# mLSTM value strips of the second block as seven block products, with strip and token sums mostly on GpSimd

## The chip, the cores and the metric

One core of one Trainium2 chip runs the whole program. The metric is the device time of one execution in microseconds (us). TensorE (PE in the rows) multiplies matrices and writes PSUM banks, ScalarE (ACT) does activation functions and copies out of PSUM, VectorE (DVE) does elementwise work, GpSimd (POOL) does elementwise work in SBUF and issues some DMAs, SyncE (SP) issues the weight DMAs.

## The reference, cut to what matters

Two blocks in a row; the first is not touched. In the second, the token mixer projects 256 context and 256 latent tokens (1024 features each) with one wide matrix and feeds the columns to two recurrences, mLSTM and HGRN2.

```python
def _token_mix(xc, xl, w_in, b_in, m_gain, lb, h_gain, proj_m, proj_h, w_out, need_ctx):
    seg_c = _split_proj(xc @ w_in + b_in)
    seg_l = _split_proj(xl @ w_in + b_in)
    hm_c, hm_l = _mlstm_branch(seg_c[0:6], seg_l[0:6], m_gain, xl.dtype)   # q, k, v, o, input gate, forget gate
    hh_c, hh_l = _hgrn_branch(seg_c[6:10], seg_l[6:10], lb, h_gain, xl.dtype)

# _mlstm_scan, one chunk: v enters here
    num = w_inter[..., None] * jnp.einsum('bhtd,bhdv->bhtv', qc, C) + jnp.einsum('bhts,bhsv->bhtv', s, vc)
```

There are 8 heads with 128 value columns each. The change is in `x @ w_in + b_in` for the 1024 value columns `v`, all in float32.

## The kernel before, in words

Every engine runs a list of instructions written out by hand, in order; semaphores (`S.…`) hold an engine until another has counted them up. `p.next` and `p.inc` keep the counts while the program is built. There is no scheduler. A float32 matmul of the program is two MATMUL instructions in the rows, each with its weight load, so counts in the profile are twice those in the code.

**The mLSTM phase** runs over four pairs of heads (`PAIRS`, counted from pair 0). For a pair four weight strips are loaded by SyncE: slot `W[0]` holds q and k, `W[1]` the 256 value columns `M_V`, `W[2]` the output gate, `W[3]` a gate strip of the other recurrence. A load waits for `S.done[r]`, which TensorE counts when it has read slot `r`. `U` holds the normalised tokens with features on the partitions: columns 0 to 255 latent, 256 to 511 context; `UP` is the latent part in column-major order.

TensorE's order in a pair is: `project` (q, k), `columns` of the pair before, `project_values`, then `remember` (scores, output gate tile 0, the state products, output gate tile 1, sums of head 0, gate strip, sums of head 1). The state products need `MV`, the biased values (`S.mv`), and `sums(h)` needs the decay tables `EE` (`S.e_ready`). In pair 0 `gate_columns` stands between the values and the scores; it transposes the gate rows `G4` and stops TensorE until VectorE has copied them (`S.tg_ready`).

**Values before:** 4 token tiles x 8 feature tiles, tokens stationary, 256 weight columns moving, into both halves of banks 2 and 3. VectorE then adds the bias `VB` while it moves them to `MV` (two instructions).

**The gate chain** of pair 0 runs beside `project` and the values: ScalarE and VectorE turn the raw gate rows (40 partitions) into cumulative sums (scans on 8 partitions) and maxima, until VectorE counts `S.gate_m`; ScalarE then makes the three exponentials of `G4` (`S.gate_exp`). GpSimd waits for that with four DMAs of gate rows to DRAM and the DMAs that broadcast them back into `WBN` and `WBX`, used by VectorE's `arguments`.

**Seven products.** The same trick that the change applies to the values already stands in other phases: for a strip split in 2 x 2 blocks (`part(t, h)`: output half t, feature half h), four weight sums (`WSR[0..3]`) and four token sums (`TBR[0..3]`) make seven block products do the work of eight. ScalarE must copy partial results out of a bank (`S.snap`) before TensorE adds a later product on top, and VectorE puts the parts together. `steps_f` of the phase after (the recurrence) does it with these buffers; its sums are made by GpSimd (weights) and by `token_sums` on VectorE (tokens, called once after pair 1).

Of the kernel before, what the change touches and what calls it, by code (L numbers as in the profile page):

```python
# [13 lines left out]
P = 128  # L14
# [242 lines left out]
def first_and_second_block(nc, a, out):  # L257
# [4 lines left out]
    with ctx:  # L262
# [168 lines left out]

        GMS, GHS = (v.rearrange("p a b c -> p (a b c)") if len(v.shape) == 4 else v.rearrange("p c d t x -> p (c d t x)")
# [39 lines left out]
        def permuted_and_context(h, c):  # L472

            return (UP[:, 4 * h:4 * h + 4, 0:SEQ], U[:, 4 * h:4 * h + 4, SEQ:2 * SEQ])[c]

# [255 lines left out]
        def _(eng):  # L731
# [665 lines left out]
            def project_values():  # L1397
                token_tiles(1, [(2, 0, toks(0)), (2, SW, toks(P)), (3, 0, toks(2 * P)), (3, SW, toks(3 * P))], (2, 3))
# [73 lines left out]
            p.leave("memory")  # L1472
            project(first=True)
            project_values()
# [165 lines left out]
            places["sums"] = (p.now(S.prod), p.now(S.wsum))  # L1640
# [76 lines left out]
        def _(eng):  # L1717
# [119 lines left out]

            eng.wait_ge(S.gate_exp, p.next(S.gate_exp))
# [5 lines left out]
            for i in range(PAIRS):  # L1844
                if i > 1:
                    eng.wait_ge(S.wb_used, p.next(S.wb_used))
# [3 lines left out]
                for h in range(2):  # L1850
                    src = rows_dram[1, 2 * i + h, :, :].rearrange("d x -> (d x)").partition_broadcast(DH)
                    eng.dma_start(WBX[i % 2][DH * h:DH * h + DH, :, :].rearrange("p d x -> p (d x)"), src).then_inc(sem, p.inc(sem, 16))

            p.meet("recurrence")
            prod, wsum = places["sums"]
            p.skip(S.prod, prod - p.now(S.prod))
            p.skip(S.wsum, wsum)
            for n in range(2 * PAIRS):
                r = n % 2
                part = lambda t, h: W[r][:, 4 * h:4 * h + 4, t * P:(t + 1) * P]  # L1860
                eng.wait_ge(S.land[r], p.next(S.land[r], 16))
                for o, x, y, op, used in ((0, part(1, 0), part(1, 1), ALU.add, 2), (1, WSR[0], part(0, 0), ALU.subtract, 2),
                                          (3, part(0, 1), WSR[1], ALU.subtract, 1), (2, part(0, 0), part(1, 0), ALU.subtract, 1)):
                    if n:
                        eng.wait_ge(S.prod, p.next(S.prod, used))
                    eng.tensor_tensor(WSR[o], x, y, op).then_inc(S.wsum, p.inc(S.wsum))  # L1866
                    eng.wait_ge(S.wsum, p.now(S.wsum))
# [3 lines left out]
        def _(eng):  # L1871
# [433 lines left out]
            act(GI[both, :], bank[6][both, :], ACT.Identity, bias=P2[both, B_IF:B_IF + 1]).then_inc(S.gate_in, p.inc(S.gate_in))  # L2305
            eng.wait_ge(S.gate_m, p.next(S.gate_m))
# [3 lines left out]
            eng.wait_ge(S.gate_exp, p.now(S.gate_exp))  # L2310

# [36 lines left out]
            for i in range(PAIRS):  # L2348
# [193 lines left out]
        def _(eng):  # L2542
# [623 lines left out]
            eng.memset(MV[:, :, :, P:VW], 1.0)  # L3166
            eng.memset(C0[:, :, :, :], 0.0).then_inc(S.order_dve, p.inc(S.order_dve))
# [54 lines left out]

            def arguments(i):
# [8 lines left out]
            for i in range(PAIRS):  # L3232
# [13 lines left out]
                ins.then_inc(S.mv, p.inc(S.mv))  # L3246
                eng.wait_ge(S.mv, p.now(S.mv))
                eng.sem_inc(S.free[2], 1)
                eng.sem_inc(S.free[3], 1)
# [303 lines left out]
```

## Time and profile before

| | us |
|---|---|
| three runs: lowest, median, highest | 1972.21, 1975.35, 1975.98 |
| the profiled execution: its own time | 1971.99 |
| the profiled execution: span of the core | 1970.2 |
| TensorE busy in the span | 1945.2 |
| VectorE, ScalarE, GpSimd busy | 1241.7, 565.9, 218.7 |

The span is the time from the core's first to its last instruction in the trace; the execution's own time is 1.8 us longer. All rows of the trace give times from the start of that span. An engine that is busy 99% of the span can still be the wrong place to look in one stretch: what matters is which wait ends last there.

### The profile page before, as it was taken

To read this page: it belongs to the slowest core of one execution; us is meant where nothing else is said; L and a number is where in the kernel's file an instruction comes from. 1 tells how busy PE (TensorE), PEld (TensorE's weight loads), DVE (VectorE), ACT (ScalarE), POOL (GpSimd) and SP (SyncE) were. 2 spreads that over 40 slices of the span, in tenths; PEclk is the share of its full clock that TensorE was granted. 3 is DMA by queue.
4 is the path that set the end of the run, shared out by engine and by line. 5 is a ranking of instruction groups with operands and counts; after the bars stand their busy time and mean duration, and the time that the engine had idled before them with its cause. 6 is when DMAs were issued, how large, how long until landed. Compare 5 with 4: busy or idle time off the path is not lost.

```text
span 1970.2 us, 31165 instructions
## 1 busy us (share of the span) xinstructions
PE 1945.2 (99%) x12449; PEld 1751.1 (89%) x12449; DVE 1241.7 (63%) x2513; ACT 565.9 (29%) x1363; POOL 218.7 (11%) x267
## 2 busy tenths in 40 slices
PE   9999999999999999999999999999999999999998
PEld 7878999977799998888888888888888989999998
DVE  5425897572378865899669565343456765766664
ACT  3343332224533313111110013322343323132212
POOL 6100430312014200000000001001212100000000
PEclk9999999999999999999999999999999999999999
DMA  6354555343545542555545364332222224545552
GB/s 199 112 187 137 165 165 161 111 151 114 172 150 171 182 140 79 182 166 164 166 152 173 116 190 136 119 90 86 86 65 67 83 67 148 172 134 167 171 177 81
DMA packets 272105, 273.60 MB, mean 139 GB/s; under 512 B 7982, under 2 KB 269338, under 8 KB 271962
## 3 DMA queue, kind: packets, MB, share of 16 engines
q1 hardware_dynamic: 270152, 267.65, 42.5%
q0 software_dynamic: 1216, 3.32, 0.6%
q8 instruction: 99, 1.62, 0.4%
q10 hardware_dynamic: 594, 0.65, 0.1%
q14 instruction: 44, 0.36, 0.1%
HBM read 270.38 MB, written 1.08 MB: 138 GB/s over the span
## 4 chain that ended last, share of the span: by engine, by line
PE 93%; DVE 4%; ACT 1%; issue 1%; DMA 1%; ACTq 0%; DVEq 0%; SPq 0%; PEldq 0%
PE bank L818 50%; PE bank L1324 10%; PE bank L796 8%; PE bank L1510 5%; PE bank L1559 2%; PE bank L966 2%; PE bank L1087 1%; PE bank L1610 1%; PE bank L1037 1%; PE bank L1494 1%; PE bank L1572 1%; PE bank L1046 1%; PE bank L1391 1%; PE bank L1235 1%; PE bank L1241 1%
## 5 line engine op out<-in xcount | busy, mean ns | idle before, releaser
L818 PE MATMUL bank<-arena,SQ 128*128 128x136 f32 (+2 forms) x2176 | 341.4, 308 | 0.1
L818 PEld LDWEIGHTS bank<-arena,SQ 128*128 128x128 f32 x2176 | 307.0, 191 | 17.2 <-ACT arena L1931 0.3
L818 PE MATMUL bank<-arena,W 128*128 128x136 f32 (+2 forms) x1824 | 272.6, 301 | 2.7 <-issue 2.1
L818 PEld LDWEIGHTS bank<-arena,W 128*128 128x128 f32 x1824 | 247.6, 191 | 15.4 <-issue 4.1
L1931 ACT ACTIVATE H<-bank 128x128 f32<-128x128 f32 (+1 forms) x260 | 82.3, 317 | 535.5 <-PE bank L818 535.5
L818 PE MATMUL bank<-U,W 128*128 128x136 f32 (+2 forms) x1296 | 194.6, 303 | 0.0
L818 PEld LDWEIGHTS bank<-U,W 128*128 128x128 f32 x1296 | 176.4, 191 | 11.0 <-issue 2.9
L796 PE MATMUL bank<-U,W 128*128 128x272 f32 (+1 forms) x576 | 133.1, 392 | 1.4 <-ACT U L2213 0.8
L3033 DVE SCALAR_TENSOR_TENSOR W<-W,CC 128x256 f32<-128x256 f32 x280 | 128.3, 483 | 7.0
L796 PEld LDWEIGHTS bank<-U,W 128*128 128x128 f32 x576 | 109.0, 190 | 24.6 <-issue 2.3
L818 PE MATMUL bank<-arena 128*128 128x136 f32 (+1 forms) x1024 | 124.1, 278 | 0.0
L818 PEld LDWEIGHTS bank<-arena 128*128 128x128 f32 x1024 | 120.6, 191 | 0.0
L1324 PE MATMUL bank<-W,U 128*128 128x256 f32 (+1 forms) x512 | 100.5, 355 | 0.0
L818 PE MATMUL bank<-U,SQ 128*128 128x136 f32 (+2 forms) x608 | 98.2, 304 | 0.0
L1931 ACT ACTIVATE arena<-bank 128x136 f32<-128x136 f32 x176 | 49.3, 280 | 168.9 <-PE bank L818 168.9
L1324 PEld LDWEIGHTS bank<-W,U 128*128 128x128 f32 x512 | 86.8, 190 | 11.5 <-issue 2.0
L818 PEld LDWEIGHTS bank<-U,SQ 128*128 128x128 f32 x608 | 85.9, 191 | 4.1
L1822 POOL TENSOR_TENSOR SQ<-W 128x512 f32<-128x512 f32 x32 | 40.7, 1273 | 267.9 <-PE bank L818 267.9
L1866 POOL TENSOR_TENSOR W<-W 128x512 f32<-128x512 f32 x32 | 41.7, 1302 | 255.4 <-PE bank L1510 170.7
L2932 DVE SCALAR_TENSOR_TENSOR arena<-arena,PL 128x270 f32<-128x270 f32 x72 | 62.7, 871 | 2.6
L1842 POOL DMA_DIRECT2D gate_rows<-arena x4 | 2.1, 540 | 528.7 <-ACT arena L2309 528.7
L2121 ACT ACTIVATE arena<-arena,PL 128x272 f32<-128x272 f32 x80 | 41.8, 522 | 64.5 <-DVE arena L2781 56.6
(459 smaller groups left out, 3117.9 us busy)
## 6 DMA issues: line engine op xcount, KB each, us to landing
W<-in_ffn_w_up_dram SPq DMA_DIRECT2D x44, 1024.0 KB, 5.1
W<-in_ffn_w_in_dram SPq DMA_DIRECT2D x44, 1024.0 KB, 5.1
W<-in_ada_w_dram SPq DMA_DIRECT2D x36, 1024.0 KB, 6.6
W<-in_mix_w_in_dram SPq DMA_DIRECT2D x36, 1024.0 KB, 5.3
W<-in_ffn_w_down_dram SPq DMA_DIRECT2D x16, 1408.0 KB, 6.6
W<-in_ffn_w_out_dram SPq DMA_DIRECT2D x16, 1408.0 KB, 6.3
W<-in_w_in_dram SPq DMA_DIRECT2D x21, 1024.0 KB, 5.3
W<-in_w_out_dram SPq DMA_DIRECT2D x8, 1024.0 KB, 8.5
```

Source lines behind the costliest of these rows:

```text
L796: last = mm(bank[b][0:m, 0:n], W[r][:, kk, t * P:t * P + m], rhs(kk), start=kk == 0, stop=kk == k - 1)
L818: last = mm(o, a(k), b[:, k], start=not adds and k == 0, stop=k == kt - 1, skip_group_check=True)
L966: return mm(bank[2 * (r % 2) + t][:, c0:c0 + n], W[r][:, k, t * P:(t + 1) * P], rhs(k), start=k == 0, stop=k == KD - 1, skip_group_check=True)
L1324: last = mm(o, x, y, start=i == 0, stop=i == n - 1 and bias is None, skip_group_check=True)
L1510: ins = mm(o, x, y, start=clear and k == 0, stop=k == 3, skip_group_check=True)
L1559: last = mm(bank[b][:, c:c + SW], tok(k), W[r][:, k, :], start=k == 0, stop=k == KD - 1, skip_group_check=True)
L1822: eng.tensor_tensor(WS[n % 2][:, 0], part(1, 0), part(1, 1), ALU.add).then_inc(S.order_pool, p.inc(S.order_pool))
L1866: eng.tensor_tensor(WSR[o], x, y, op).then_inc(S.wsum, p.inc(S.wsum))
L1931: act(sn[:, i, :], bank[b][:, c:c + w], ACT.Copy).then_inc(S.snap, p.inc(S.snap))
L2121: act(CZ[:, 2 * s + t, :], Z[:, g % 2, 2 * s + t, :], ACT.Copy, scale=PLs[l][:, c:c + 1]).then_inc(S.tap, p.inc(S.tap))
L2932: stt(CZ[:, i, 2:], Z[:, g % 2, i, 0:T1 - 2], w(0), CZ[:, i, 2:], ALU.mult, ALU.add).then_inc(sem, p.inc(sem))
L3033: ins = stt(o, x, c, o, ALU.mult, ALU.add) if k else ts(o, x, c, None, ALU.mult)
```

## The change

Each of the four calls of `project_values` becomes seven block products. A block product is 4 feature tiles x 2 token tiles, tokens stationary, 128 weight columns moving: 56 matmuls of 128 columns for 32 of 256. The raw value copies `SNV` (made by ScalarE in `kept_values`) get their bias on VectorE and are then added to what stands in the banks. The weight sums of the value strips, and three of the four token sums, are made by GpSimd; the first token sum of all is VectorE's, ahead of the gate chain. The token sums of the recurrence move from VectorE (after pair 1) to GpSimd (after pair 3). The diff, shortened:

```diff
+        SNV = [SQ[:, 4 + i // 2, (i % 2) * SEQ:(i % 2 + 1) * SEQ] for i in range(4)]
+        SNV_LATE = SQ[:, 5, :].rearrange("p (a b) -> p a b", a=2)
...
-            def project_values():
-                token_tiles(1, [(2, 0, toks(0)), (2, SW, toks(P)), (3, 0, toks(2 * P)), (3, SW, toks(3 * P))], (2, 3))
+            def project_values(first=False):
...
+                def product(b, c, tok, w, clear=False, release=False):
+                    for k in range(4):
+                        for n in range(2):
+                            last = mm(bank[b][:, c + n * P:c + (n + 1) * P], tok[:, k, n * P:(n + 1) * P], w[:, k],
+                                      start=clear and k == n == 0, stop=k == 3, skip_group_check=True)
+                        if release and k == 0:
+                            last.then_inc(S.done[1], p.inc(S.done[1]))
+                    return last
...
+                product(2, near, latent_and_context(0, 0), raw(0, 0), True).then_inc(S.prod, p.inc(S.prod))
+                take(3)
+                token_sum()
+                eng.wait_ge(S.wsum, p.next(S.wsum))
+                product(3, near, TBR[0], WSR[0], True).then_inc(S.prod, p.inc(S.prod))
+                eng.wait_ge(S.snap, p.next(S.snap))
+                product(2, far, latent_and_context(1, 0), raw(0, 1))
+                eng.wait_ge(S.snap, p.next(S.snap))
+                token_sum(2)
+                product(3, far, TBR[3], raw(1, 1)).then_inc(S.prod, p.inc(S.prod))
...
             project(first=True)
-            project_values()
+            project_values(True)
...
+            def strip_sums(r, which=(0, 1, 3, 2), first=False):
...
+            eng.wait_ge(S.done[3], p.next(S.done[3]))
+            strip_sums(1, (0,), True)
+            eng.wait_ge(S.tsum, p.next(S.tsum))
+            token_sum(1, latent_and_context(1, 1), TBR[0])
+            token_sum(3, latent_and_context(1, 0), TBR[1])
+            strip_sums(1, (1, 3), True)
+            token_sum(2, latent_and_context(1, 1), latent_and_context(0, 1))
+            strip_sums(1, (2,), True)
             eng.wait_ge(S.gate_exp, p.next(S.gate_exp))
...
             for i in range(PAIRS):
                 if i > 1:
+                    strip_sums(1)
                     eng.wait_ge(S.wb_used, p.next(S.wb_used))
...
+            strip_sums(1)
+            eng.wait_ge(S.prod, p.now(S.prod) + 6)
+            eng.tensor_tensor(TBR[0], permuted_and_context(0, 1), permuted_and_context(0, 0), ALU.subtract).then_inc(S.order_pool, p.inc(S.order_pool))
...
+            kept_values((0,))
             eng.wait_ge(S.gate_m, p.next(S.gate_m))
...
             eng.wait_ge(S.gate_exp, p.now(S.gate_exp))
+            kept_values((1,))
...
                 eng.sem_inc(S.free[0], 1)
+                kept_values((0, 1, 2, 3) if i else (2, 3))
...
+            tt(TBR[0], latent_and_context(0, 1), latent_and_context(0, 0), ALU.subtract).then_inc(S.tsum, p.inc(S.tsum))
...
-                eng.wait_ge(S.done[1], p.next(S.done[1]))
-                vb = VB[:, i * SW:(i + 1) * SW].rearrange("p (b c) -> p b c", b=2).unsqueeze(1).to_broadcast([P, 2, 2, P])
-                for n in range(2):
-                    ins = tt(MV[:, 2 * n:2 * n + 2, :, 0:P], bank[2 + n][:, :].rearrange("p (a b c) -> p a b c", a=2, b=2), vb, ALU.add)
+                for n, t in ((0, 0), (3, 1), (1, 0), (2, 1)):
+                    eng.wait_ge(S.snap, p.next(S.snap))
+                    bias = VB[:, i * SW + t * P:i * SW + (t + 1) * P].unsqueeze(1).to_broadcast([P, 2, P])
+                    ins = tt(two_tiles(SNV[n]), two_tiles(SNV[n]), bias, ALU.add)
...
+                tt(MV[:, 2:4, 0, 0:P], two_tiles(SNV[1]), two_tiles(bank[3][:, 0:SEQ]), ALU.add).then_inc(S.order_dve, p.inc(S.order_dve))
...
+                tt(MV[:, 0:2, 0, 0:P], two_tiles(SNV[0]), two_tiles(bank[2][:, SEQ:2 * SEQ]), ALU.add)
+                both = two_tiles(bank[2][:, 0:SEQ]).unsqueeze(1).to_broadcast([P, 2, 2, P])
+                tt(MV[:, :, 1, 0:P].rearrange("p (c n) m -> p c n m", c=2), SNV_LATE.rearrange("p c (n m) -> p c n m", n=2), both,
+                   ALU.add).then_inc(S.mv, p.inc(S.mv))
...
-                if i == 1:
-                    token_sums(permuted_and_context, TBR)
...
-                r = n % 2
-                part = lambda t, h: W[r][:, 4 * h:4 * h + 4, t * P:(t + 1) * P]
...
+                strip_sums(n % 2)
```

**TensorE in pair 0**, from the last instructions of `project` to the scores (`bank<-W,U` is weights and tokens of the program; names after "waits" are semaphores). Before:

```order
L1324 MATMUL bank<-W,U 128x128 x16
L1324 MATMUL bank<-W,U 128x256 [waits free3,free2,land1]
L1324 MATMUL bank<-W,U 128x256 x31
L1366 MATMUL bank<-ident,arena 128x40 [waits free4,gate_exp]
L1366 MATMUL bank<-ident,arena 128x40 x7
L1408 MATMUL bank<-arena 128x256 [waits free4,free5,mqk,tg_ready]
```

After (of the eight instructions of each product the first stands here):

```order
L1331 MATMUL bank<-W,U 128x128 x16
L1414 MATMUL bank<-W,U 128x128 [waits free2,land1]
L1414 MATMUL bank<-W,H 128x128 [waits wsum,tsum,free3]
L1414 MATMUL bank<-W,U 128x128 [waits snap]
L1414 MATMUL bank<-W,arena 128x128 [waits tsum,snap]
L1414 MATMUL bank<-W,H 128x128 [waits wsum]
L1414 MATMUL bank<-W,U 128x128 [waits wsum]
L1414 MATMUL bank<-W,arena 128x128 [waits snap,wsum,tsum]
L1373 MATMUL bank<-ident,arena 128x40 [waits free4,gate_exp]
L1454 MATMUL bank<-arena 128x256 [waits free4,free5,mqk,tg_ready]
```

The values' one wait for slot 1 and the banks has become seven groups of eight, each with a wait of its own: on weight sums (`wsum`), token sums (`tsum`) or ScalarE's copies (`snap`). `tsum,snap` is the fourth product.

**GpSimd**, from the last strip of the first block to its DMAs of gate rows. Before:

```order
L1822 TENSOR_TENSOR SQ<-W 128x512 [waits prod,land3,first_sums]
L1824 TENSOR_TENSOR SQ<-W 128x512 [waits order_pool]
L1842 DMA gate_rows<-arena 8x256 [waits gate_exp,prod,first_sums]
L1842 DMA gate_rows<-arena 8x256 x3
L1849 DMA arena<-gate_rows 128x1024 [waits wrow]
L1852 DMA arena<-gate_rows 64x512 x2
L1849 DMA arena<-gate_rows 128x1024
```

After (`H<-U,H`, `arena<-U,H` and `arena<-U` are token sums of 1024 elements, `W<-W` weight sums of 512):

```order
L1870 TENSOR_TENSOR SQ<-W 128x512 [waits order_pool]
L1904 TENSOR_TENSOR W<-W 128x512 [waits done3,land1,prod,first_sums]
L1891 TENSOR_TENSOR H<-U,H 128x4x256 [waits tsum,wsum]
L1891 TENSOR_TENSOR arena<-U,H 128x1024 [waits tsum]
L1904 TENSOR_TENSOR W<-W 128x512 [waits tsum]
L1904 TENSOR_TENSOR W<-W 128x512 [waits wsum]
L1891 TENSOR_TENSOR arena<-U 128x1024 [waits wsum]
L1904 TENSOR_TENSOR W<-W 128x512 [waits tsum]
L1919 DMA gate_rows<-arena 8x256 [waits gate_exp,wsum]
L1919 DMA gate_rows<-arena 8x256 x3
L1927 DMA arena<-gate_rows 128x1024 [waits wrow]
```

Seven sums now stand between the last strip of the first block (L1870) and the DMAs of gate rows. Further down, the four weight sums of pair 1's strip stand ahead of the DMA for pair 2.

**ScalarE in pair 0**, the gate chain's end. After the change:

```order
L2380 ACTIVATE arena<-bank,P 40x512 [waits gf_full]
L2387 ACTIVATE SQ<-bank 128x256 [waits prod]
L2393 ACTIVATE arena<-arena 40x256 [waits gate_m]
L2394 ACTIVATE arena<-arena 40x256
L2395 ACTIVATE arena<-arena 40x256
L2387 ACTIVATE SQ<-bank 128x256 [waits prod,gate_exp]
L1956 ACT_TABLE_LOAD
L2437 ACTIVATE arena<-bank,MQB 128x256 [waits done0]
L2438 ACTIVATE arena<-bank,P 128x256
L2387 ACTIVATE SQ<-bank 128x256 [waits mqk,prod]
L2387 ACTIVATE SQ<-bank 128x256 [waits prod]
```

The four copies `SQ<-bank` are new. The second of them, which the fourth product waits for, stands behind the three exponentials (40x256) and so behind `gate_m`; the last two stand behind q and k.

## Rows read from the trace of the kernel before

**Rows 1.** The page: busy time, the granted clock in 40 slices, the chain by engine

```profile
PE 1945.2 (99%) x12449; PEld 1751.1 (89%) x12449; DVE 1241.7 (63%) x2513; ACT 565.9 (29%) x1363; POOL 218.7 (11%) x267
...
PEclk9999999999999999999999999999999999999999
...
PE 93%; DVE 4%; ACT 1%; issue 1%; DMA 1%; ACTq 0%; DVEq 0%; SPq 0%; PEldq 0%
```

**Rows 2.** The chain that ended last in 1185 to 1262 us: start, us, what

```profile
1192.44 17.39 PE bank L1324 x96
1209.83 0.63 PE bank L1366 x8
...
1239.64 3.57 PE bank L1324 x32
...
1243.64 13.81 PE bank L1324 x64
```

**Rows 3.** Timeline of the merge phase: start, us, engine, line, operation, count

```profile
1648.95 1.06 PE L818 MATMUL bank<-W 128*128 128x128 f32 x8
1649.85 1.06 PE L818 MATMUL bank<-U,arena 128*128 128x128 f32 x8
```

**Rows 4.** Timeline of the gate chain in pair 0

```profile
1186.89 0.60 ACT L2295 ACTIVATE arena<-bank 128x512 f32<-128x512 f32 x1 [2.26 <-PE bank L1338]
...
1187.90 0.49 DVE L3167 MEMSET arena<- 128x516 f32 x1
...
1190.49 0.74 DVE L3170 TENSOR_SCALAR arena<-bank,P 40x512 f32<-40x512 f32 x1 [2.10 <-ACT arena L2299]
...
1191.74 0.68 DVE L3174 TENSOR_TENSOR arena<-arena 40x512 f32<-40x512 f32 x1 [0.51 <-ACT arena L2303]
...
1192.46 2.55 DVE L3181 TENSOR_TENSOR_SCAN arena<-ones_row,arena 8x256 f32<-8x256 f32 x4
1195.18 0.69 DVE L3185 TENSOR_TENSOR arena<-arena 40x512 f32<-40x512 f32 x1 [0.17 <-DVE arena L3181]
...
1199.53 0.51 ACT L2307 ACTIVATE arena<-arena 40x256 f32<-40x256 f32 x1 [7.25 <-DVE arena L3206]
...
1200.35 0.40 ACT L2309 ACTIVATE arena<-arena 40x256 f32<-40x256 f32 x1
...
1201.35 2.14 POOL L1842 DMA_DIRECT2D gate_rows<-arena  x4 [528.67 <-ACT arena L2309]
```

**Rows 5.** Timelines: elementwise work of GpSimd and a token sum of VectorE

```profile
357.11 0.73 POOL L1835 TENSOR_TENSOR HIB<-HIB 128x256 f32<-128x256 f32 x1
...
1285.54 1.22 DVE L2701 TENSOR_TENSOR H<-U,H 128x1024 f32<-128x1024 f32 x1
...
1342.13 5.29 POOL L1866 TENSOR_TENSOR W<-W 128x512 f32<-128x512 f32 x4 [80.50 <-DMA W<-in_mix_w_in_dram]
```

**Rows 6.** Timelines: VectorE and GpSimd at the same time, and VectorE alone

```profile
346.90 1.91 DVE L2764 TENSOR_TENSOR arena<-W 128x1408 f32<-128x1408 f32 x1 [0.22 <-DVE arena L2787]
...
347.41 1.99 POOL L1835 TENSOR_TENSOR HIB<-HIB 128x256 f32<-128x256 f32 x1
...
1415.64 1.30 DVE L3407 TENSOR_TENSOR_SCAN arena<-arena,ones_row 128x255 f32<-128x255 f32 x2
...
1424.39 2.30 DVE L3410 TENSOR_TENSOR_SCAN arena<-arena,ones_row 128x255 f32<-128x255 f32 x2
...
1424.68 1.46 POOL L1866 TENSOR_TENSOR W<-W 128x512 f32<-128x512 f32 x1 [23.25 <-PE bank L1510]
```

**Rows 7.** Timeline of TensorE at the start of the program

```profile
2.84 4.56 PE L747 MATMUL bank<-ident 128*128 128x128 f32 x20 [2.84 <-POOL LNT L1730]
```

**Rows 8.** Timeline behind the values of pair 0, and the landing of the load issued there (last number)

```profile
1212.64 1.28 DVE L3245 TENSOR_TENSOR arena<-bank,arena 128x512 f32<-128x512 f32 x2
...
1216.11 1.59 PE L1324 MATMUL bank<-arena 128*64 128x129 f32 x16
...
W<-in_mix_w_in_dram SPq DMA_DIRECT2D x1, 1024.0 KB, 6.2
```

More of the change, by code:

```diff
@@ L1472, in _ @@
             p.leave("memory")
+            places["sums"] = (p.now(S.prod), p.now(S.wsum), p.now(S.tsum))
             project(first=True)
-            project_values()
+            project_values(True)
             gate_columns()
@@ L1836, in _, with token_sum @@
                         eng.wait_ge(sem, p.now(sem))
+            p.meet("memory")
+            prod, wsum, tsum = places["sums"]
+            p.skip(S.prod, prod - p.now(S.prod))
+            p.skip(S.wsum, wsum)
+            p.skip(S.tsum, tsum)
+            def token_sum(o, x, y):
+                eng.tensor_tensor(TBR[o], x, y, ALU.subtract).then_inc(S.tsum, p.inc(S.tsum))
+                eng.wait_ge(S.tsum, p.now(S.tsum))
+            def strip_sums(r, which=(0, 1, 3, 2), first=False):
+                part = lambda t, h: W[r][:, 4 * h:4 * h + 4, t * P:(t + 1) * P]
+                for o in which:
+                    if o == 0:
+                        eng.wait_ge(S.land[r], p.next(S.land[r], 16))
+                    x, y, op, used = ((part(1, 0), part(1, 1), ALU.add, 2), (WSR[0], part(0, 0), ALU.subtract, 2),
+                                      (part(0, 0), part(1, 0), ALU.subtract, 1), (part(0, 1), WSR[1], ALU.subtract, 1))[o]
+                    if not first:
+                        eng.wait_ge(S.prod, p.next(S.prod, used))
+                    eng.tensor_tensor(WSR[o], x, y, op).then_inc(S.wsum, p.inc(S.wsum))
+                    eng.wait_ge(S.wsum, p.now(S.wsum))
+            eng.wait_ge(S.done[3], p.next(S.done[3]))
[6 more added lines that the diff above has]
+            strip_sums(1, (2,), True)
             eng.wait_ge(S.gate_exp, p.next(S.gate_exp))
@@ L1852, in _ @@
                     eng.dma_start(WBX[i % 2][DH * h:DH * h + DH, :, :].rearrange("p d x -> p (d x)"), src).then_inc(sem, p.inc(sem, 16))
+            strip_sums(1)
+            eng.wait_ge(S.prod, p.now(S.prod) + 6)
+            eng.tensor_tensor(TBR[0], permuted_and_context(0, 1), permuted_and_context(0, 0), ALU.subtract).then_inc(S.order_pool, p.inc(S.order_pool))
+            eng.wait_ge(S.order_pool, p.now(S.order_pool))
+            eng.tensor_tensor(TBR[1], permuted_and_context(1, 1), TBR[0], ALU.subtract).then_inc(S.order_pool, p.inc(S.order_pool))
+            eng.wait_ge(S.order_pool, p.now(S.order_pool))
+            token_sum(3, permuted_and_context(1, 0), TBR[1])
             p.meet("recurrence")
[L1855 to L1857 removed]
             for n in range(2 * PAIRS):
[L1859 to L1867 removed]
+                strip_sums(n % 2)
         @block.scalar
@@ L2305, in _, with kept_values @@
             act(GI[both, :], bank[6][both, :], ACT.Identity, bias=P2[both, B_IF:B_IF + 1]).then_inc(S.gate_in, p.inc(S.gate_in))
+            def kept_values(which):
+                x, z, y = bank[2][:, 0:SEQ], bank[3][:, 0:SEQ], bank[3][:, SEQ:2 * SEQ]
+                for n in which:
+                    eng.wait_ge(S.prod, p.next(S.prod, 2 if n == 2 else 1))
+                    i, src = ((0, x), (3, z), (1, x), (2, y))[n]
+                    act(SNV[i], src, ACT.Copy).then_inc(S.snap, p.inc(S.snap))
+                    if n == 3:
+                        p.skip(S.prod)
+            kept_values((0,))
             eng.wait_ge(S.gate_m, p.next(S.gate_m))
```

33 lines of the change are left out of this document (29 added, 4 removed).

## The prediction

> **What bounds the kernel now.** The page comes first. TensorE is busy 99% of the span and carries 93% of the chain that ended last [rows 1]. So the question in each stretch is only whether TensorE's stream gets shorter, and whether something new stops it. VectorE (63%) and GpSimd (11%) look idle enough to take any work, but these are averages; what counts is who waits for them in the stretch of the change.
>
> The chain in order of time then shows the mLSTM phase as one stream of TensorE. In pair 1 the values are 64 instructions in 13.81 us, 0.216 us each, and the 32 instructions of 128 columns before them take 3.57 us, 0.1116 us each [rows 2]. In pair 0 both kinds stand in one piece: 96 instructions in 17.39 us, from 1192.44 to 1209.83. The values of pair 0 thus begin near 1192.3 + 3.57 = 1195.85 and end near 1209.7.
>
> **What the change takes from TensorE.** A call of `project_values` becomes 112 instructions of 128 columns. The nearest rows for such block products are those of the merge phase: eight in 1649.85 - 1648.95 = 0.90 us, 0.1116 us each as above, with semaphore waits between the groups and no gap [rows 2, 3]. 112 x 0.1116 = 12.50 us for 13.81 to 13.82: 1.32 us less per call, **-5.3 us** in four calls. One block in eight is saved, but under a tenth of the time, because two instructions of 128 columns take 0.223 us where one of 256 takes 0.216.
>
> **Pair 0: sums that come before the gate chain is done.** The other places where the stream could stop are the seven new groups of waits. Pair 0 is the tight one, since the sums can't be made in an earlier pair.
>
> VectorE's first token sum (1024 elements, 1.22 us [rows 5]) stands ahead of the `MEMSET` that began at 1187.90. VectorE waited 2.10 us before 1190.49 for ScalarE [rows 4], and the sum fits into that: it costs nothing. Were the cover gone, it would be 1.2 us.
>
> GpSimd starts at about 1186.9, when `done[3]` starts ScalarE as well [rows 4]. A weight sum takes 5.29 / 4 = 1.32 us with its gap, 1.27 without [rows 5, 6]. No row shows a GpSimd sum of 1024 elements. From 0.73 us at 256 and 1.27 at 512 I work out 0.73 + 3 x 0.54 = 2.35 us; the bounds are 1.27 and 2 x 1.32 = 2.64. The order is: weight sum to 1188.2, wait for VectorE's token sum to 1189.4, token sum to 1191.8, then 2.35 + 1.27 + 1.27 + 2.35 + 1.27 = 8.5 us more, to 1200.8. By themselves all are in time for TensorE: products 2 to 7 follow in steps of 16 x 0.1116 = 1.79 us, the fourth at 1195.85 + 3 x 1.79 = 1201.2, the seventh at 1206.6.
>
> But GpSimd's sums run exactly while VectorE works on the gate chain, and the rows show that the two hold each other up. Two scans take 1.30 us alone, and 2.30 us when a GpSimd sum of 1.27 us asks during the first: it got in between the two though VectorE had no wait there. A GpSimd operation of 0.73 us took 1.99 us beside a VectorE operation with two SBUF inputs [rows 5, 6]. So they alternate, one operation each, at +1.00 us for a sum of 1.27 us, that is its duration less 0.27. From 1191.74 VectorE has six operations that read two SBUF tiles: one `TENSOR_TENSOR`, four scans, one `TENSOR_TENSOR` (L3174, L3181, L3185) [rows 4]. That is five gaps for GpSimd's five sums. Delay: 8.5 - 5 x 0.27 = 7.15 us; the first may be partly hidden in VectorE's own wait, I take 7.0. Bounds: 0 if these operations, on 40 and 8 partitions, don't collide (every case in the rows has 128), and 8.5 + 0.6 if nothing overlaps.
>
> Here a rule is weighed against the rows. The Trainium skill, page "SBUF — State Buffer", section "Who interferes with whom", says that a VectorE instruction with two SBUF inputs and a GpSimd instruction that reads SBUF contend for a shared port, held for the whole instruction. Nothing in it depends on the number of partitions. By the rule the delay is the 7 us above; by the rows alone it lies between 0 and 9. The rule speaks against this change, and the trace agrees with it as far as it goes.
>
> **What waits for the gate chain.** Before, ScalarE's exponentials started at 1199.53 and ended at 1200.75; only the gate DMAs and the transposes behind the values needed them [rows 4]. Now the copy of bank 3 (`kept_values((1,))`) stands behind them on ScalarE, and the fourth product waits for it. With the chain 7.0 us late the copy ends at 1200.75 + 7.0 + 0.4 = 1208.15 (0.4 us as the last exponential). TensorE, in order, is at that product at 1201.2. **+7.0 us** of stop, with products 4 to 7, transposes and scores queued behind. Without the collision the copy would be ready at 1201.15, and the stop nothing.
>
> **The clock after the stop.** TensorE has not stood still for as long as this anywhere but at the program's start. There, behind 2.84 us without work, 20 instructions of 128 columns took 4.56 us, 0.228 us each, twice the 0.1116 of later: the 1.2 GHz level for the 2.4 GHz level [rows 7]. (The granted-clock line prints its highest digit in all slices and does not resolve this [rows 1].) If the stop brings the clock down in the same way and 4.4 us of work follow at the lower level, half of that is lost: **+2.2 us**. Bounds: 0 if it stays up, 7.1 us (products 4 to 7 at double) if it stays down for all four. The Trainium skill, page "TensorE: Matmul & The Clock Gate", Part 1, calls the throttled state the default that activity releases; by it the clock falls, and the sum holds the 2.2 us, without it the sum is 2.2 us less.
>
> **Behind the values of pair 0.** VectorE has four bias additions on SBUF, two additions of 256 and one of 512 elements where it had two of 512 in 1.28 us [rows 8]. From 0.42 us for the first and 0.34 for each that follows, about 1.7 + 0.5 + 1.1 = 3.3 us: `MV` is ready 2.0 us later than before against the end of the values. It was ready at 1213.9, TensorE took it at 1216.11 [rows 8]: slack 2.2 us, cost 0, by a hair. In pairs 1 to 3 the four additions are made while the products still run, so nothing is later than before.
>
> GpSimd's gate DMAs leave 7 us later than 1201.35 [rows 4], but the values end later by more than 6 as well; their users follow `MV`. Cost 0.
>
> **Pair 3 and the recurrence.** Three token sums (7.1 us) and four weight sums (5.3 us) begin at the end of pair 3's values, about 1344 in the new time, and end near 1357. The recurrence wants them from about 1372. Cost 0; the four token sums taken from VectorE (4.9 us at 1285.54 [rows 5]) give nothing, as no engine waited for them.
>
> **The sum.** -5.3 + 7.0 + 2.2 = **+3.9 us** on the profiled execution's 1971.99 us, 1975.9. The runs shown have their median 3.4 us above that execution, so on their scale 1975.35 + 3.9 = **1979.2 us**. A measurement of this kernel can tell about 0.2% from no change, 3.95 us: the forecast lies on that line, from below.
>
> **Rivals.**
> 1. *No collision in the gate chain* (operations on few partitions don't block, or GpSimd always loses and keeps its slack of 5.8 us before the seventh product). For it: no row shows a blocked operation with fewer than 128 partitions. Against: the scans on 128 alternate. Only the -5.3 us are left: 1970.1, faster. The turning point is a delay of 5.3 us with the clock up, of 3.1 with it down. Chance 0.22.
> 2. *The stop, but the clock stays up*: -5.3 + 7.0 = +1.7, 1977.1. Chance 0.13.
> 3. *A short stop* of 1 to 5 us without the clock's fall, because VectorE often gets in twice running: -4 to 0. Chance 0.05, counted as no change.
> 4. *A second collision at `MV`*. The strip of pair 1 is asked for in the last product, about 1.1 us before the values end, and lands 6.2 us later [rows 8], so 5.1 us behind the end. The additions run from 3 to 6 us behind it. If it lands a little earlier, up to three of them wait one weight sum each: +1 to +3.8 us on the likeliest case, 1981 to 1983. The same chance holds a clock that stays down for longer. Chance 0.15.
>
> The likeliest case has 0.45, its own range is +2.7 to +5.6 us (a 1024-element sum of 1.9 to 2.6 us, 1.5 to 3.4 us for the clock). Half of it lies over 0.2%. Faster: 0.22. Slower: 0.22 + 0.15 = 0.37. Same: 0.41. The range reaches from rival 1 to rival 4: 1969.5 to 1983.5.
>
> **What the new profile would show.** Block products of the values at 0.11 us each, 12.5 us from first to last in pairs 1 to 3, with no gap. In pair 0, one idle time of about 7 us before a group that reads `W` and `arena` (the fourth product), put down to ScalarE; the scans, 2.55 us before, spread over 8 us or more with GpSimd's sums between them; the first instructions behind the stop at 0.22 us. If the scans still take 2.55 us, rival 1 is right. If TensorE waits at the state products (`bank<-arena` 128x129), rival 4 is. The forecast would be wrong altogether if GpSimd's sums of 1024 elements took far longer than 2.6 us, or if the block products ran slower than in the merge phase.

## The result, and the profile after

The changed kernel takes 1976.57 us (median of 19 runs, 1975.65 to 1980.6), the kernel before 1972.38 us beside it (19 runs, 1971.85 to 1975.98): ratio 1.002 [1.0013, 1.0028]. It is slower by 4.2 us; the interval leaves out 1, so the loss is real, and it is about 0.2%. The profiled execution has a span of 1974.6 us, 4.4 more than before.

The page of the changed kernel, as in [rows 1]:

```profile
PE 1942.4 (98%) x12641; PEld 1755.4 (89%) x12641; DVE 1263.2 (64%) x2530; ACT 572.0 (29%) x1379; POOL 257.6 (13%) x289
...
PE 94%; DVE 2%; ACT 1%; DMA 1%; issue 1%; ACTq 0%; DVEq 0%; SPq 0%; PEldq 0%
```

TensorE has 2.8 us less work, and VectorE 21.5 us more although it lost token sums and gained only small additions. The additions explain little of it: they take 2.9 us for 1.28 in each pair, and of the token sums 1.2 us came and 4.9 us left, 3 us more in all. That is the first sign: operations that were there before became longer.

Timeline of pair 0, the stretch of [rows 4] (start, us, engine, line, operation). L3265, L3272, L3276 are the two-input operations and scans of the gate chain, L1904 and L1891 GpSimd's strip and token sums, L2387 the copies on ScalarE, L1414 the block products:

```profile
1187.32 3.11 POOL L1904 TENSOR_TENSOR W<-W 128x512 f32<-128x512 f32 x1 [514.50 <-PE bank L1345]
...
1188.10 1.21 DVE L3256 TENSOR_TENSOR H<-U 128x1024 f32<-128x1024 f32 x1
...
1190.51 2.37 POOL L1891 TENSOR_TENSOR H<-U,H 128x1024 f32<-128x1024 f32 x1
...
1192.04 1.39 DVE L3265 TENSOR_TENSOR arena<-arena 40x512 f32<-40x512 f32 x1 [0.51 <-ACT arena L2378]
...
1192.96 2.68 POOL L1891 TENSOR_TENSOR arena<-U,H 128x1024 f32<-128x1024 f32 x1
1193.46 8.63 DVE L3272 TENSOR_TENSOR_SCAN arena<-ones_row,arena 8x256 f32<-8x256 f32 x4
1195.72 3.14 POOL L1904 TENSOR_TENSOR W<-W 128x512 f32<-128x512 f32 x2
...
1198.94 2.61 POOL L1891 TENSOR_TENSOR arena<-U 128x1024 f32<-128x1024 f32 x1
...
1201.63 1.53 POOL L1904 TENSOR_TENSOR W<-W 128x512 f32<-128x512 f32 x1
...
1202.27 1.43 DVE L3276 TENSOR_TENSOR arena<-arena 40x512 f32<-40x512 f32 x1 [0.17 <-DVE arena L3272]
...
1207.36 0.51 ACT L2393 ACTIVATE arena<-arena 40x256 f32<-40x256 f32 x1 [8.84 <-DVE arena L3297]
...
1208.61 0.38 ACT L2387 ACTIVATE SQ<-bank 128x256 f32<-128x256 f32 x1
1209.04 3.78 PE L1414 MATMUL bank<-W,arena 128*128 128x128 f32 x16 [7.37 <-ACT SQ L2387]
...
1212.62 2.05 PE L1414 MATMUL bank<-W,H 128*128 128x128 f32 x16
1214.50 1.95 PE L1414 MATMUL bank<-W,U 128*128 128x128 f32 x16
```

Read it from below. The fourth product waited 7.37 us, for the copy at 1208.61. The copy stood behind ScalarE's exponentials, which started at 1207.36 where they had started at 1199.53. They waited for VectorE, whose four scans took 8.63 us instead of 2.55, and the operations before and after them 1.39 and 1.43 us instead of 0.68 and 0.69. GpSimd worked all that time. (The trace lies 0.3 us later than that of before from the start of this stretch.)

The last four products of pair 0, behind the stop, and the seven of pair 1, which run freely (the chain, as in [rows 2]):

```profile
1209.04 9.19 PE bank L1414 x64
...
1252.05 12.51 PE bank L1414 x112
```

The balance: 13.81 - 12.51 = 1.30 us saved in each pair; in pair 0 the transposes behind the values begin at 1218.17 instead of 1209.76, which is 8.1 us later after the 0.3. So +8.1 - 3 x 1.30 = +4.2 us.

### The profile page after: what moved, and what is told of

The parts are those of the page before. It is cut to its first block, busy times and chain, and to the rows that moved or that the text cites. A ratio compares the mean times of both kernels' runs of the same rounds, so it can differ in the third digit from the quotient of the medians.

```text
span 1974.6 us, 31636 instructions
## 1 busy us (share of the span) xinstructions
PE 1942.4 (98%) x12641; PEld 1755.4 (89%) x12641; DVE 1263.2 (64%) x2530; ACT 572.0 (29%) x1379; POOL 257.6 (13%) x289
## 3 DMA queue, kind: packets, MB, share of 16 engines
q0 software_dynamic: 1216, 3.32, 0.5%
## 4 chain that ended last, share of the span: by engine, by line
PE 94%; DVE 2%; ACT 1%; DMA 1%; issue 1%; ACTq 0%; DVEq 0%; SPq 0%; PEldq 0%
PE bank L825 52%; PE bank L803 9%; PE bank L1331 7%; PE bank L1557 5%; PE bank L1606 3%; PE bank L1414 2%; PE bank L973 2%; PE bank L1657 2%; PE bank L1044 1%; PE bank L1541 1%; PE bank L1094 1%; PE bank L1619 1%; PE bank L1053 1%; PE bank L1242 1%; PE bank L1248 1%; PE bank L1398 1%
## 5 line engine op out<-in xcount | busy, mean ns | idle before, releaser
L1904 POOL TENSOR_TENSOR W<-W 128x512 f32<-128x512 f32 x48 | 65.2, 1358 | 756.1 <-PE bank L1345 514.5
L825 PE MATMUL bank<-arena,U 128*128 128x256 f32 (+1 forms) x352 | 59.2, 327 | 0.4 <-DVE U L2852 0.4
L1557 PE MATMUL bank<-H,W 128*128 128x256 f32 x256 | 58.9, 379 | 0.7 <-ACTq L2471 0.7
L825 PEld LDWEIGHTS bank<-arena,U 128*128 128x128 f32 x352 | 53.5, 191 | 5.2 <-DVE U L2852 0.6
```

The lines of the kernel that those rows point to most:

```text
L825: last = mm(o, a(k), b[:, k], start=not adds and k == 0, stop=k == kt - 1, skip_group_check=True)
L1557: ins = mm(o, x, y, start=clear and k == 0, stop=k == 3, skip_group_check=True)
```

## The experiments

All medians below have the kernel before measured beside them (1972.1 to 1972.4 us); each ratio is to it.

**Theory A**, the prediction's: GpSimd's sums stretch VectorE's gate chain, ScalarE's copy waits for it, TensorE for the copy, and the clock falls. The rivals are lettered B, C and so on; a letter does not mean the same in every experiment, and each expectation says what it stands for.

### 1. The clock: work for TensorE in the stop

```diff
                 product(2, far, latent_and_context(1, 0), raw(0, 1))
+                if first:
+                    keep_busy(bank[5][:, 0:P], 28)
```

> 28 matmuls (56 instructions of 128 columns) that nobody reads stand between the third and the fourth product of pair 0, 56 x 0.1116 = 6.2 us of work inside a stop of 7.4 us. Theory A with the clock as the price of the stop: the idle time shrinks to about 1.2 us, the granted clock stays at 1.00, the products behind run at 0.112 us each: 1.9 us under the changed kernel, 2.3 us over the kernel before. Rival (the 0.22 us per instruction behind the stop belongs to these products, not to the clock): they stay slow and the time is that of the changed kernel.

Measured: 1974.49 us (11 runs), ratio 1.0012 [1.0003, 1.002], 2.1 us under the changed kernel. Windows of the changed kernel (stretch, its length, busy time and instructions of PE, PEld, DVE, ACT and POOL, then the granted clock as a share of 2.4 GHz, the DMA share and GB/s):

```profile
1183.00:1201.00 18.00, 18.00 (x127) 14.62 (x126) 16.06 (x28) 5.42 (x11) 13.29 (x6) 1.00 0.39 114
1201.00:1207.50 6.50, 0.68 (x7) 0.48 (x5) 5.88 (x13) 0.14 (x1) 2.08 (x2) 0.88 0.05 12
1207.50:1209.00 1.50, 0.00 (x0) 0.00 (x0) 0.00 (x0) 1.46 (x4) 0.00 (x0) 0.50 0.00 0
1209.00:1211.00 2.00, 1.96 (x9) 1.96 (x10) 0.00 (x0) 1.98 (x3) 1.85 (x4) 0.50 0.04 8
1211.00:1216.00 5.00, 5.00 (x39) 5.00 (x39) 0.00 (x0) 0.53 (x2) 3.57 (x7) 0.82 0.39 125
```

and of the kernel with the filler:

```profile
1201.00:1208.00 7.00, 6.56 (x59) 6.37 (x58) 5.52 (x13) 1.00 (x3) 1.70 (x2) 1.00 0.02 4
1208.00:1213.00 5.00, 4.32 (x38) 4.33 (x39) 0.00 (x0) 3.10 (x6) 2.83 (x6) 1.00 0.03 7
```

Without work the clock went to its 1.2 GHz level (0.50) during the stop, and stayed there for the first group behind it: 3.78 us for 16 instructions, then 2.05, then 1.95. With the filler it stayed at 2.4 GHz and the last four products took 7.41 us in one piece instead of 9.19. The clock's term is shown, and the rival falls: the same products ran at full speed. The copy that they wait for comes no earlier than before, so the rest of the loss stays.

### 2. One more sum on GpSimd

```diff
+            eng.tensor_tensor(TBR[1], latent_and_context(1, 1), TBR[0], ALU.subtract).then_inc(S.order_pool, p.inc(S.order_pool))
+            eng.wait_ge(S.order_pool, p.now(S.order_pool))
             token_sum(1, latent_and_context(1, 1), TBR[0])
```

> GpSimd makes the second token sum of pair 0 twice (2.37 us more of GpSimd work beside the gate chain). Theory A: the stop grows by 2.37 less 0.3 to about 9.5 us, the clock's loss stays: 2.1 us over the changed kernel, 6.3 us over the kernel before. Theory C: no change against the changed kernel, since the sums have 4 us of slack before the product that reads them.

Measured: 1977.64 us (7 runs), ratio 1.0027 [1.0016, 1.0038]: 1.1 us over the changed kernel, half of what theory A said. The timeline says why:

```profile
1201.32 2.60 POOL L1891 TENSOR_TENSOR arena<-U 128x1024 f32<-128x1024 f32 x1
1201.96 2.51 DVE L3278 TENSOR_TENSOR arena<-arena 40x512 f32<-40x512 f32 x1 [0.18 <-DVE arena L3274]
...
1204.00 1.59 POOL L1904 TENSOR_TENSOR W<-W 128x512 f32<-128x512 f32 x1
...
1209.89 3.78 PE L1414 MATMUL bank<-W,arena 128*128 128x128 f32 x16 [8.51 <-ACT SQ L2389]
```

VectorE has six operations beside which a sum can get in. The extra sum takes one place, and the last sum (1.27 us by itself) falls behind the sixth, where it delays next to nothing: 2.35 - 1.27 = 1.1 us. The stop grew by as much, from 7.37 to 8.51 us; the medians alone, with intervals that overlap, would not carry this. Theory C, no change at all, does not fit the longer stop. It is the prediction's alternation; my expectation forgot that its places are few.

### 3. The sums without their size

```diff
-                eng.tensor_tensor(TBR[o], x, y, ALU.subtract)
+                eng.tensor_tensor(cut_to(TBR[o]), cut_to(x), cut_to(y), ALU.subtract)
```

`cut_to` takes `v[:, :, 0:1]`, and the strip sums of pair 0 are cut alike, as is one token sum of the recurrence. Every wait stays; two products that read a token sum in the change read tokens here, and one of the recurrence reads another token sum. A first version, which left the operands of these products as they were, gave no time.

> The changed kernel with the sums of the mLSTM stage cut to their first element of each 128, all their waits kept (its values are therefore not the reference's): the collision is gone, everything else of the change stays. Theory A/D: the gate exponentials end near 1201, no stop before the fourth product of more than 0.5 us, the gate rows are as early as before, and all four value groups give 1.31 us each: 1972.3 - 5.3 = 1967.0 us (1966.5 to 1968). Rival B (the stop comes from the copy's place behind the gate exponentials, collision or not): a stop of 1 to 2 us and a lower clock stay, 1969 to 1971 us. Rival C (the saving is not there): 1971 us or more.

Measured: 1967.34 us (7 runs), ratio 0.9973 [0.9962, 0.9984]. The scans took 2.55 us again, and all seven products of pair 0 stand in one piece of the chain (the first line is from the timeline):

```profile
1194.39 2.55 DVE L3274 TENSOR_TENSOR_SCAN arena<-ones_row,arena 8x256 f32<-8x256 f32 x4
...
1197.95 12.61 PE bank L1414 x112
```

So the loss goes with the length of the sums. The waits, the copy's place, the longer additions and the seven products themselves leave 0.3 us by the medians, which these runs do not resolve (the interval is 2.2 us wide on each side), and 0.1 us in the trace, where the seven products take 12.61 us for 12.51 in pair 1. Rivals B and C of this experiment fall.

### 4. The copies first

```diff
-            kept_values((0,))
+            kept_values((0, 1, 2, 3))
             eng.wait_ge(S.gate_m, p.next(S.gate_m))
...
             eng.wait_ge(S.gate_exp, p.now(S.gate_exp))
-            kept_values((1,))
...
-                kept_values((0, 1, 2, 3) if i else (2, 3))
+                if i:
+                    kept_values((0, 1, 2, 3))
```

> In pair 0 all four of ScalarE's copies of the values stand ahead of its wait for the gate chain, so no product waits for the chain; the sums on GpSimd stay. Theory A (GpSimd's sums hold up VectorE's operations with two SBUF inputs, and the copy behind the chain hands that delay to TensorE): the four scans stay stretched to 8 to 9 us, the stop of 7.4 us before the fourth product goes, and with it the slow clock; perhaps 0.3 us before the transposes and 0.4 us before the scores, since q and k are copied later. Time 4.7 us under the kernel before, 8.9 us under the changed one. Theory B (the products themselves, or the token sums as operands, are slow in pair 0): the fourth product still starts late or runs at 0.22 us per instruction, and the time stays within 2 us of the changed kernel.

Measured: 1971.48 us (11 runs), ratio 0.9992 [0.9983, 1.0001]. The stop before the fourth product is gone, and the product runs at full speed, so this experiment's rival B falls. But of the 5.3 us only 0.7 are there, and the expected 4.7 us were missed. The chain shows another path, through the gate rows that go to DRAM and come back to VectorE's exponent arguments (L3322):

```profile
1211.33 2.60 DMA gate_rows<-arena
...
1215.34 4.75 DMA arena<-gate_rows
...
1220.12 3.95 DVE arena L3322 x8
```

and its timeline, GpSimd's strip sums and the first head's sums of TensorE:

```profile
1217.46 5.53 POOL L1904 TENSOR_TENSOR W<-W 128x512 f32<-128x512 f32 x4
...
1226.73 4.11 PE L1331 MATMUL bank<-arena 128*128 128x129 f32 x20 [1.94 <-DVE arena L3369]
```

TensorE stopped 1.94 us before the first head's sums and ran them at a low clock (0.58 granted over 1226.7 to 1230.8 us), 4.11 us for 2.40; with 0.45 us more before the scores that is 4.1 of the 4.6 us that were missing. Two things made it late: the gate rows, whose first transfer was issued at 1209.70 instead of 1201.35, 7.5 us later after the 0.8 us by which this trace lies later, and GpSimd's strip sums of pair 1, which the change put ahead of its next transfers and which ran beside the arguments. Theory A had neither; a theory D took the first.

### 5. The same collision in the kernel before

```diff
+            part = lambda t, h: U[:, 4 * h:4 * h + 4, t * P:(t + 1) * P]
...
+            extra(WSR[0], part(1, 0), part(1, 1), ALU.add)
+            eng.wait_ge(S.extra, 1)
+            extra(TBR[1], u(1, 1), TBR[0], ALU.subtract)
+            extra(TBR[3], u(1, 0), TBR[1], ALU.subtract)
...
             eng.wait_ge(S.gate_exp, p.next(S.gate_exp))
```

The strip sums have their size but read tokens here, not weights.

> The kernel before, with VectorE's first token sum and GpSimd's seven sums of pair 0 added at their places and sizes (four strip sums of 512 elements, three token sums of 1024); nobody reads them and no matrix product waits for them. All readings say that VectorE's gate chain is stretched by some 7.5 us, so that the gate exponentials end near 1208.5 in place of 1200.8 while the tokens-stationary values end at 1209.8. Theory A (the prediction's: the delay costs only through the ScalarE copy behind it, which this kernel does not have): no change, 1972.3 us within 1. Theory D (from the run with the copies first: the same delay has a second victim, the gate rows that go through DRAM to VectorE's exponent arguments, and with them the first head's sums): the arguments start near 1219.5 in place of 1214.2, TensorE stops 2 to 2.4 us before the first head's sums and loses another 1.7 to the clock, 1975.8 to 1976.4 us.

Measured: 1973.03 us (11 runs), ratio 1.0003 [0.9994, 1.0012]. The timeline (L3201 are the scans, L3248 the arguments, L1325 the first head's sums):

```profile
1192.99 8.64 DVE L3201 TENSOR_TENSOR_SCAN arena<-ones_row,arena 8x256 f32<-8x256 f32 x4
...
1219.53 1.92 DVE L3248 TENSOR_SCALAR arena<-arena 128x256 f32<-128x256 f32 x8 [5.07 <-DMA arena<-gate_rows]
...
1225.18 2.40 PE L1325 MATMUL bank<-arena 128*128 128x129 f32 x20
```

Its scans took 8.64 us and its exponentials began at 1206.94, so the gate chain was as late as in the changed kernel, and the time did not change beyond its interval. Theory D falls. Its late rows came as worked out (arguments at 1219.53), but the arguments took 1.92 us here, since the kernel before has no strip sums there, and the masks were ready at 1224.02 for a TensorE that came free at 1225.2. So experiment 4's stop needed both late rows and strip sums beside the arguments, and a TensorE that is not itself 8 us late: theory E, which the next experiment tests.

### 6. Those strip sums later, three times

First, on the kernel of experiment 4, they go behind the gate row transfers of pair 2:

```diff
                 if i > 1:
-                    strip_sums(1)
+                    if i > 2:
+                        strip_sums(1)
                     eng.wait_ge(S.wb_used, p.next(S.wb_used))
...
+                if i == 2:
+                    strip_sums(1)
```

> The version with all four ScalarE copies of pair 0 ahead of the gate exponentials, and one thing more: GpSimd makes pair 1's strip sums behind its gate row transfers of pair 2, about 1226, instead of ahead of them, 1217 to 1223. Theory E (the stop before the first head's sums in that version needed two things, gate rows late by the stretched chain and VectorE's arguments stretched from 1.92 to 3.95 us by those strip sums; the kernel before with the sums alone had only the first and no stop): arguments back at 1.92 us, masks ready about 1224.6 on that version's scale where TensorE comes free at 1224.8, no stop and no slow clock there, 3.5 to 4 us less than 1971.5: 1967.5 us (1967.2 to 1968.4). Rival F (the late gate rows alone make the stop): the arguments cannot begin before 1220, so at least 1.9 us of it stays, 1969.5 to 1971.5 us.

Measured: 1971.96 us (11 runs), ratio 1.0 [0.9991, 1.0009]; no gain, and outside what either theory had given. The first stop is gone as theory E said, and a second stands in its place (timeline; L3372 are the masks):

```profile
1222.77 2.28 DVE L3372 TENSOR_TENSOR arena<-arena,tri 128x256 f32<-128x256 f32 x2
1223.47 5.46 POOL L1904 TENSOR_TENSOR W<-W 128x512 f32<-128x512 f32 x4
...
1226.37 2.84 DVE L3372 TENSOR_TENSOR arena<-arena,tri 128x256 f32<-128x256 f32 x2
...
1233.43 3.51 PE L1331 MATMUL bank<-arena 128*128 128x129 f32 x20 [2.08 <-DVEq L3408]
```

The strip sums now ran beside the masks (0.76 us for each two of them alone), and the second head's sums were late.

Second, on top of this, the second token sum goes from GpSimd to VectorE, behind the first one:

```diff
+            tt(TBR[1], latent_and_context(1, 1), TBR[0], ALU.subtract).then_inc(S.tsum, p.inc(S.tsum))
```

> The previous version of this call, with the second token sum (the tokens' difference from the first) on VectorE at once behind the first, in the time in which it waits for the gate projection, instead of on GpSimd. GpSimd's row of sums is one of 2.4 us shorter, so the gate chain is stretched by some 5 us instead of 7.5, and ends near 1206. Theory E: the wait of 0.45 us before the score products goes too and the first head's sums have some 2 us to spare: 1967.0 us, 0.2 to 0.6 below the previous version, at the edge of what five rounds tell. Rival F: 1.5 to 2.5 us below the previous version, since the stop that it sees in the late rows shrinks with the chain.

Measured: 1972.65 us (11 runs), ratio 1.0001 [0.9992, 1.001], no better. The gate chain did end 0.7 us earlier, but the exponentials did not start earlier (1207.09 for 1207.14): with the four copies first, ScalarE's last copy waits for the sixth product at 1206.8. And the sum took 2.17 us on VectorE, beside GpSimd's strip sum. Neither theory had seen that. TensorE stopped 2.36 us before the second head's sums here too.

Last, GpSimd waits until VectorE has finished pair 0's first head:

```diff
                 if i == 2:
+                    eng.wait_ge(S.hm, 1)
                     strip_sums(1)
```

> The version with the four copies first, with pair 1's strip sums later still: GpSimd waits for VectorE to finish the first head of pair 0 (about 1232) before it makes them, 1232 to 1238; they are needed at 1248. Both earlier places cost the same 4 us: at 1217 to 1223 they stretched the exponent arguments (stop before the first head), at 1223 to 1229 the masks (0.76 to 2.28 and 2.84 us; stop of 2.1 us before the second head, and a low clock behind it). Theory E2 (every one of those stops is the late gate chain plus the strip sums beside VectorE's two-input operations; without the second there is none): arguments 1.92, masks 0.76 each, no stop before either head, 1967.5 us (1967.1 to 1968.6), level with or just below the version with pairs 1 to 3 only. Rival F2 (the late gate rows alone are enough to stop the second head's sums, or the sums behind 1232 make the stop before the columns' transposes): 1969.5 us or more.

Measured: 1968.86 us (11 runs), ratio 0.9984 [0.9975, 0.9993]: 3.1 us less than the first placing of this series, with nothing changed but the time of four sums. It lies 0.3 us over E2's range and below F2's. The two heads (timeline):

```profile
1224.63 2.47 PE L1331 MATMUL bank<-arena 128*128 128x129 f32 x20 [0.35 <-issue]
...
1230.83 2.47 PE L1331 MATMUL bank<-arena 128*128 128x129 f32 x20 [0.28 <-DVEq L3409]
```

Theory E2 is right in kind. Some 1.5 us of small waits stay: from the last 32 instructions of pair 0's `project` to those of pair 1's, the chain takes 47.43 us here and 47.20 in the kernel before, where the saving alone would give 45.90. Of these, 0.45 us lie before the scores and about 0.5 at each head's sums. The late rows make VectorE's chain the bound there, so F2 holds for that part.

### 7. The change without pair 0

```diff
             def project_values(first=False, sums_new=False):
+                if first:
+                    token_tiles(1, [(2, 0, toks(0)), (2, SW, toks(P)), (3, 0, toks(2 * P)), (3, SW, toks(3 * P))], (2, 3))
+                    return
```

Pair 0's copies and GpSimd's sums go, its biases are added as before; VectorE makes three token sums behind the gate chain. Pair 1's strip sums stand behind the gate row transfers of pair 2, as in the first placing of experiment 6.

> A version meant to beat both: pair 0 computes its values as before (four token tiles, biases added in one step), pairs 1 to 3 by the seven products. GpSimd does nothing beside the gate chain; VectorE makes the token sums, the first at its place and three behind the gate chain where it waits 11 us for the transposes; GpSimd makes pair 1's strip sums behind its first gate row transfers of pair 2. Theory A/D: no stop in pair 0, three times 1.31 us saved, 1972.3 - 3.9 = 1968.4 us (1967.8 to 1969.2). Rival: GpSimd's strip sums, now at 1218 to 1224, stretch VectorE's decay products and make the first head's sums late: 1970 us or more. Rival C (the saving of the seven products is eaten in pairs 1 to 3 too): 1971 to 1972.5 us.

Measured: 1968.18 us (11 runs), ratio 0.9978 [0.9969, 0.9986]. This beats both kernels, the one before by 4.2 us and the changed one by 8.4. Three pairs of 1.30 us make 3.9 of the 4.2. GpSimd's strip sums stretched the masks in pair 0 here too (2.29 and 2.85 us), but nothing waited (timeline):

```profile
1218.53 5.47 POOL L1908 TENSOR_TENSOR W<-W 128x512 f32<-128x512 f32 x4
...
1221.44 2.85 DVE L3383 TENSOR_TENSOR arena<-arena,tri 128x256 f32<-128x256 f32 x2
...
1224.58 2.40 PE L1331 MATMUL bank<-arena 128*128 128x129 f32 x20
```

> The version with seven products in pairs 1 to 3 only, its strip sums of pair 1 at the same later place. There its gate chain is early, so the masks that they stretched at 1218 to 1224 (2.29 and 2.85 us in place of 0.76) stopped nothing. Theory E2: same time as that version, 1968.2 us within 0.5. Rival (the stretched masks cost it something, through a late release of banks): 0.5 to 1 us less.

Measured, with `eng.wait_ge(S.hm, 1)` before those sums: 1968.11 us (11 runs), ratio 0.9977 [0.9967, 0.9986], the same. With an early gate chain the place of these sums is free.

## Why the prediction was right

It gave +3.9 us on the profiled execution; that became +4.4 in span and +4.2 in the medians. The mechanism it named is the one that the traces show; two of its terms came out as they did partly by luck (the clock's size and the gate DMAs, below). By its steps:

- **The saving**, -1.32 us a call: measured 1.30 in each of pairs 1 to 3, and -5.0 for all four in experiment 3. Right.
- **The collision**, 7.0 us by alternation of one operation each: the last of the six operations counted (L3276) ended at 1203.70 instead of 1195.87, 7.5 us later after the 0.3. The 1024-element sum took 2.37 us for an estimated 2.35. The doubt whether operations on 40 and 8 partitions collide is settled: they do, as those of 128. The Trainium skill, "SBUF — State Buffer", "Who interferes with whom", states the contention for a VectorE instruction with two SBUF inputs, without a condition on partitions; the trace agrees, with a scan on 8 partitions that went from 0.64 us to 2.2 us on average. Experiment 3 shows that the loss goes with the length of the sums, and experiment 2 that the chain has few places for them.
- **Where the 0.5 us more came from.** VectorE's first token sum was put at nothing, because VectorE waits there; that wait did cover it. But GpSimd's first strip sum ran beside it and took 3.11 us where 1.27 was taken. The second sum began at 1190.51 where 1189.4 was worked out, 0.8 us later after the 0.3, and so still held up L3265 (1.39 us for 0.68). The five sums of the prediction's account delayed the other five operations by 6.8 us, for its 7.15.
- **The stop**, +7.0: 7.4. Its path, through the copy behind the exponentials, was the one named; experiment 4 removed just this link, and the stop went.
- **The clock**, +2.2: 2.0 (9.19 - 7.14 us), and 2.1 by experiment 1. The estimate took 4.4 us of slow work from the program's start. That this would carry over to a stop in mid-stream no row had shown; the size is a lucky hit.
- **Costs put at nothing.** The additions before `MV`: it was ready at 1224.09, TensorE took it at 1224.52, so 0.4 us of slack were left; right, by a hair. Rival 4's collision there did not come: the strip sums began at 1223.55, after the four additions on SBUF; the last three additions have one input in PSUM, and the one beside which the sums began took 0.68 us, as in experiment 3 without them. The strip sums hit the arguments behind it instead (5.48 us for 1.93), and no stop of TensorE followed, for TensorE was itself 8 us late.
- **The gate DMAs**, cost 0, was right only because the stop hid them. "Their users follow `MV`" was the reason given, and it was thin: once the stop is gone (experiments 4 and 6) late rows and strip sums together took 4.6 to 5.2 us of the 5.3. The number 0 held for this kernel, the reason for it did not.
- **The recurrence's sums**, cost 0: right, with other times than given. They ran from 1354.07 to 1367.26, not from 1344 to 1357 (the sum of the prediction itself puts the end of pair 3's values near 1353), and the recurrence wanted them at 1379.34.
- **The likeliest case's range.** Its lower end does not come out of its own terms: two sums at 1.9 us take 0.9 us off the 7.0, and -5.3 + 6.1 + 1.5 is +2.3, not +2.7.
- **The scale.** The median of the three runs shown, 1975.35, lay 3 us over the 1972.38 of 19 runs, so the forecast on its scale, 1979.2 us, was 2.6 us too high. By the profiled execution's own scale the forecast was 1975.9; the measured median is 1976.57. The range given, 1969.5 to 1983.5, would have held rival 1's outcome as well, so it is the steps that bear out the mechanism and not the time.

Open: the last placing in experiment 6 should by its own small waits have given 1972.36 - 5.2 + 1.5 = 1968.7 us; the 0.2 us to the measured 1968.86 are below what these runs resolve. A version with seven products in all four pairs and none of the collisions was not made; by experiment 3 it could give about 0.8 us more than experiment 7.

## What to carry to other kernels

An engine at 11% is free on average and may still be the costliest to use, if its work falls beside another engine's dependent chain: ask which chain of short operations runs at that moment, and add, for each of its operations that collide, one GpSimd operation less the overlap (0.27 us in the prediction, 0.29 on average at the four scans). Moving such work by a few microseconds, or leaving the change out in the one tight repetition and keeping it in the others, was worth more here than any repair of the order on the engine that was seen to wait. And a stop hides others behind it: after taking one away, read the chain again before counting the gain.

## What the runs showed of the hardware

- Scans on 8 partitions are held up like full ones: two of them took 4.33 us instead of 1.3.
- Not only operations with two SBUF inputs suffered. Eight `TENSOR_SCALAR` from SBUF to SBUF took 1.92 us alone and 3.95 to 5.48 us beside GpSimd's sums (5.77 us in experiment 2); the prediction had not counted them. The decay products, whose second input lies in PSUM, took 1.14 us with and without (experiment 7, during the strip sums), and the gate chain's `TENSOR_REDUCE` 0.41 us with and without (experiment 2, during the last strip sum). The Trainium skill, "SBUF — State Buffer", "Who interferes with whom", lists `tensor_scalar` among those that can contend and `tensor_reduce` and a single SBUF input among those that do not; the traces agree.
- GpSimd can lose too. Its first strip sum took 3.11 us, though it began 0.78 us before VectorE's token sum of 1.21 us. In experiment 3 it took 2.04 us there with 4 elements, and ended as VectorE's ended. In experiment 5 it was 1.30 us, and VectorE's 1.55. What decides is open; two `MEMSET` of VectorE start within 0.1 us of it in each case.
- A wait of 1.4 us before the scores was followed by a low clock once (first placing of experiment 6: granted clock 0.73 over 1212 to 1216 us, 4.52 us for a group of 3.72), and not in experiment 4 nor in the two other runs with the same wait. So a stop of this length cost either nothing or some 1.7 us.
